# DeltaNet block inversion: the unknown begun as the identity on the chip, and the inverse kept row first in memory

## What is computed

```
A = where(strict, einsum('bhnid,bhnjd->bhnij', kb, k) * decay, 0.0)
eye = jnp.eye(C)
rhs = concatenate([v * beta, kb * exp(g)], -1)
sol = triangular_solve(eye + A, rhs, left_side=True, lower=True, unit_diagonal=True)
```

## Time and profile before

| | us |
|---|---|
| median of 3 runs | 952.81 |
| the three runs | 952.17, 952.81, 958.84 |
| span of the profiled execution, first to last instruction | 950.6 |
| DeltaNet heads 0 to 7, first join (L1472) of head 0 to that of head 7 | 428.98 to 718.35 |
| mean granted clock of TensorE over the span | 0.888 of full speed |

### The profile page before, as it was taken

How to read it: one execution, slowest core, us unless ns; L and a number is a source line. 1 busy time by engine, 2 the same in 40 slices (tenths; PEclk the granted TensorE clock), 3 DMA queues, 4 the chain that set the end, 5 groups by cost and what they waited for, 6 DMA issues and landing times. The chain is left out here.

```text
span 950.6 us, 14976 instructions
## 1 busy us (share of the span) xinstructions
PE 775.6 (82%) x5209; PEld 466.6 (49%) x5209; DVE 429.6 (45%) x1039; ACT 336.3 (35%) x776; POOL 290.3 (31%) x694
## 2 busy tenths in 40 slices
PE   0978869999999178999998989989987646999970
PEld 0644425555555024456656666656655333555540
DVE  0039543212122583634765767665844652112116
ACT  0231322322222225534755556464631121322221
POOL 0000112333333100455272735537260012333330
PEclk9989959999999569986998999997997757999995
DMA  9999999999791798657242351523210199999913
GB/s 234 406 375 400 407 382 380 383 366 336 258 378 57 308 362 246 204 157 227 40 117 67 89 140 33 140 44 113 46 50 7 62 408 360 361 379 385 374 69 124
DMA packets 115874, 220.47 MB, mean 232 GB/s; under 512 B 44631, under 2 KB 78751, under 8 KB 104801
## 3 DMA queue, kind: packets, MB, share of 16 engines
q1 hardware_dynamic: 106847, 201.56, 61.0%
q0 software_dynamic: 8224, 15.75, 4.9%
q10 hardware_dynamic: 740, 2.32, 0.8%
HBM read 213.27 MB, written 17.33 MB: 243 GB/s over the span
## 5 line engine op out<-in xcount | busy, mean ns | idle before, releaser
L1200 PE MATMUL banks<-h_cols,weight_ring 128*128 128x512 f32 (+1 forms) x384 | 166.7, 556 | 0.8
L809 DVE TENSOR_TENSOR arena<-arena,banks 128x128 f32<-128x128 f32 x42 | 12.1, 287 | 203.7 <-ACT arena L780 203.7
L867 POOL DMA_INDIRECT y_of_tokens<-arena,place_now x42 | 44.0, 1048 | 169.7 <-ACT arena L787 169.7
L1200 PEld LDWEIGHTS banks<-h_cols,weight_ring 128*128 128x128 f32 x384 | 69.8, 205 | 35.6 <-issue 32.0
L1182 POOL TENSOR_TENSOR arena<-arena 128x60 f32<-128x60 f32 (+10 forms) x240 | 78.7, 328 | 18.8
L1180 POOL TENSOR_TENSOR arena<-arena 128x60 f32<-128x60 f32 (+10 forms) x240 | 76.5, 319 | 18.8
L287 PE MATMUL banks<-weight_ring,c_cols 128*32 128x512 f32 x368 | 53.0, 694 | 27.8 <-DMA weight_ring<-in_w_mod_dram 27.8
L845 POOL DMA_INDIRECT arena<-h_of_tokens,row_now x50 | 49.2, 984 | 85.9 <-DVE place_of_slot L714 38.0
L775 ACT COPY arena<-arena 64x1024 f32<-64x1024 f32 x46 | 48.1, 1045 | 77.1 <-PE banks L733 56.8
L752 PE MATMUL banks<-weight_ring,arena 128*64 128x256 f32 x576 | 67.6, 389 | 1.1 <-ACT arena L775 1.1
L733 PE MATMUL banks<-const,arena 64*128 64x64 f32 x352 | 57.1, 285 | 13.1 <-ACT arena L775 13.1
(11 more groups left out here) (294 smaller groups left out, 1395.2 us busy)
## 6 DMA issues: line engine op xcount, KB each, us to landing
weight_ring<-in_w_mod_dram SPq DMA_DIRECT2D x46, 1024.0 KB, 9.5
weight_ring<-in_dn_w_in_dram SPq DMA_DIRECT2D x32, 512.0 KB, 7.1
weight_ring<-in_w_gate_dram SPq DMA_DIRECT2D x13, 1024.0 KB, 11.1
weight_ring<-in_w_up_dram SPq DMA_DIRECT2D x13, 1024.0 KB, 14.4
weight_ring<-in_w_down_dram SPq DMA_DIRECT2D x13, 1024.0 KB, 16.1
arena<-in_w_gate_dram SPq DMA_DIRECT2D x7, 1024.0 KB, 11.5
arena<-in_w_up_dram SPq DMA_DIRECT2D x7, 1024.0 KB, 14.0
arena<-in_w_down_dram SPq DMA_DIRECT2D x7, 1024.0 KB, 15.4
```

The costliest lines, as they stand in the source:

```text
L867: pool.indirect_dma_start(y_halves, bass.IndirectOffsetOnAxis(m.place_now[:, u:u + 1], 0), v.y_tile[u], None, bounds_check=last_row, oob_i ...
L1200: mm = pe.matmul(bank(6 + j % 2)[:, 0:CTX + SEQ - n0], head_w[h % 2][:, j, k, :], m.hT[:, k, n0:CTX + SEQ], start=(k == 0), stop=(k == KD ...
```

## The change

U is no longer loaded: GpSimd copies the identity (in U's layout) into it, after the previous head's U has been written out and before it waits for the loads, which are now four. The elimination runs over columns 0 to 30 rather than 1 to 30, so that it begins with the identity and ends as the inverse: 31 pairs instead of 30, with q = j // 4 + 1 row groups instead of (j - 1) // 4 + 1. The mask and the closing subtraction are gone. The inverse lies in memory as (block, row, system, column) instead of (system, block, row, column), so that the load of W_diag reads one run of 1 KB for each partition. The mask leaves the constants, which shrink from 16 to 14 column blocks of 64 KB.

```diff
-C_STRICT, C_EYE = 11, 13
+C_EYE = 11
-C_SLOT = 15
-N_CONST = 16
+C_SLOT = 13
+N_CONST = 14
...
-        w_dram = nc.dram_tensor("inverted_blocks", (SYS, NB, BLK, BLK), F32).ap()
+        w_dram = nc.dram_tensor("inverted_blocks", (NB, BLK, SYS, BLK), F32).ap()
...
         def sp_blocks_in(sp, h):
             sp.wait_ge(s("n_out"), 16 * (h + 1))
-            sp.dma_start(U, n_dram.rearrange("s k (q g) c -> g (s k) q c", g=4)).then_inc(s("m_in"), 16)
             for g in range(4):
                 sp.dma_start(M[g * BLK:(g + 1) * BLK, :, :], n_dram.rearrange("s k r c -> (s k) r c")).then_inc(s("m_in"), 16)
 
         def sp_inverse_out(sp, h):
             sp.wait_ge(s("block_step"), STEPS * (h + 1))
-            sp.dma_start(w_dram.rearrange("s k (q g) c -> g (s k) q c", g=4), U).then_inc(s("u_out"), 16)
+            sp.dma_start(w_dram.rearrange("k (q g) s c -> g s k q c", g=4), U).then_inc(s("u_out"), 16)
...
-            sp.dma_start(W_diag, w_dram.rearrange("s k r c -> (k r) s c")).then_inc(s("w_base"), 16)
-
-        STEPS = 2 + 2 * (BLK - 2)
+            sp.dma_start(W_diag, w_dram.rearrange("k r s c -> (k r) s c")).then_inc(s("w_base"), 16)
+
+        STEPS = 1 + 2 * (BLK - 1)
...
-            pool.wait_ge(s("m_in"), 80 * (h + 1))
-            then(pool.tensor_tensor(U, U, v.strict_rows, ALU.mult))
-            for j in range(1, BLK - 1):
-                q = (j - 1) // 4 + 1
+            if h >= 1:
+                pool.wait_ge(s("u_out"), 16 * h)
+            then(pool.tensor_copy(U, v.eye_rows))
+            pool.wait_ge(s("m_in"), 64 * (h + 1))
+            for j in range(BLK - 1):
+                q = j // 4 + 1
                 part = U_part[:, 0:q, 0:BLK - 1 - j]
                 then(pool.tensor_tensor(part, U[:, 0:q, j:j + 1].to_broadcast([P, q, BLK - 1 - j]),
                                         M[:, j, j + 1:BLK].unsqueeze(1).to_broadcast([P, q, BLK - 1 - j]), ALU.mult))
-                then(pool.tensor_tensor(U[:, 0:q, j + 1:BLK], U[:, 0:q, j + 1:BLK], part, ALU.subtract))
-            pool.tensor_tensor(U, v.eye_rows, U, ALU.subtract).then_inc(s("block_step"), 1)
+                ins = pool.tensor_tensor(U[:, 0:q, j + 1:BLK], U[:, 0:q, j + 1:BLK], part, ALU.subtract)
+                if j < BLK - 2:
+                    then(ins)
+                else:
+                    ins.then_inc(s("block_step"), 1)
...
-                sp.wait_ge(s("m_in"), 80 * (x + 2))
+                sp.wait_ge(s("m_in"), 64 * (x + 2))
```

More of the change, by code:

```diff
@@ L114, in columns @@
     v.lower_in = c[:, C_LOWER_IN * P:(C_LOWER_IN + 1) * P]
-    v.strict_rows = c[:, C_STRICT * P:(C_STRICT + 2) * P].rearrange("p (q n) -> p q n", q=8)
     v.eye_rows = c[:, C_EYE * P:(C_EYE + 2) * P].rearrange("p (q n) -> p q n", q=8)
@@ L2319, in constants @@
     row = 4 * (np.arange(2 * P)[None, :] // 32) + i // 32
-    put(C_STRICT, np.arange(2 * P)[None, :] % 32 > row)
     put(C_EYE, np.arange(2 * P)[None, :] % 32 == row)
```

## The result

| | before | changed |
|---|---|---|
| median, us | 952.49 (4 runs) | 927.88 (4 runs: 927.07 to 931.07) |
| ratio of the runs | | 0.9732, interval 0.97 to 0.9764 |
| span of the profiled execution | 950.6 | 929.2 |
| same, five more rounds: median | 954.05 (9 runs) | 929.29 (5 runs), ratio 0.9728, 0.9702 to 0.9755 |

Faster by 24.6 us, where 18.4 were forecast.

The account below looks back on a forecast made before the run. Bound: the inversion's turn through SP, memory and GpSimd, just above TensorE's need. Head 2 3.2, four stretches 13.5, last stretch 1.4, constants 0.3: 18.4 us off span 950.6, 932.2, plus 2.2: 934.4 us; 8-in-10 range 931.5 to 944.5.

Parts of the forecast that it names:

- The saving per turn: Inversion loop, from one N_diag write to the next, 41.07 us in head 2: 3.2 us less forecast.
- The load of U: SP's loads before GpSimd starts: dropping U's issue saves 0.6 us and M's hold 1.8, together 2.4 per turn.
- The hold: One M load issue per head held to 2.4 us, blamed on U's 1024 small pieces filling the queue: 1.82 us.
- the upper bound: Load of U, at most 3.5 us saved per turn, if M also lands faster, by 1.1 us.
- Rival 1: M, not U, lands late; the 2.4 us hold is M's own: 1.4 saved per turn, 943.4 us, chance 0.13.
- GpSimd: 0.4 forecast: Elimination per turn: mask and subtraction gone, one pair and wider row groups added, 0.6 saved, less 0.2 for VectorE's disturbance.
- W_diag's 0.4: Back-load of W_diag in 128 runs of 1 KB for 1024 of 128 B: 0.4 us saved per turn.
- The floor of TensorE: Stretch between joins: TensorE alone needs 37.9 us; 38.15 with VectorE's floor, 38.3 with a residue.
- The 0.25 for VectorE's extra work: Steps 3 to 6: VectorE's transposes finish at 552.2, 0.25 us after TensorE is ready for the join.
- "Saving more than 3.5 per turn brings only 1 us more": Whole kernel: beyond 3.5 us saved per turn TensorE is the bound, so only 1 us more is gained.
- Rival 4: Clock still falls after 1 us waits, or GpSimd slows: two or three stretches stay at 40, 940 us, chance 0.09.
- A step that no row shows: Write of U in the new layout, 4.86 us to SP's next issue: 0 saved, bounds 0 and -2.7.

Follow-up runs that it names:

- the dead load: Changed kernel with U's removed load put back, issued ahead of M's four into U_part, which GpSimd overwrites: 935.9 us, ratio 0.9833.
- the changed kernel's second profile: The changed kernel run again with no edit, five more rounds: ratio 0.9728 against the kernel before, span 923.4 us.

## Why the prediction was wrong, and where it was right

**The saving per turn otherwise.** The load of U: 3.06 us for 2.4 forecast, and its mechanism as told. The hold belonged to U's load (back with the dead load, gone without), and M also landed faster after its last issue (2.8 us to GpSimd's start in head 2, from 3.8), which I had in the upper bound alone. So GpSimd started 4.1 us after SP's first M, where I had named 4.5 to 5.5. Rival 1 fell with it. GpSimd: 0.4 forecast, -0.10 measured. Counting instructions was not enough: the time from GpSimd's start to U's write did not get shorter. In head 7, beside a quieter VectorE, it is 24.2 before and 23.8 after, but 24.1 in the changed kernel's second profile and 23.7 in the kernel with the new layout alone, whose GpSimd work is the old one. So no gain of GpSimd is shown, and why it is missing stays open. W_diag's 0.4 is real (2.1 us to landing, from 2.5), but I put it into the turn, where SP does not wait for it.

**The floor of TensorE.** I took 37.9 us, plus 0.25 and a residue, for what TensorE needs, and called 38.3. It was 37.1 to 37.6. The 37.9 held a wait of 0.28 us inside it, for VectorE, which was late since the decay rows were queued behind SP's wait for M; with M early that went too, and 0.3 to 0.5 us more for which no row names a cause. I had listed those loads as going out 2 to 3 us earlier, and gave them no gain. The 0.25 for VectorE's extra work was right: the joins of heads 3 to 6 wait 0.2 to 0.4 us.

**How it adds up.** With a write of 4.8 us the turn is 38.2 to 38.9 and still just above TensorE: 936.5, a saving of 1.9% where 18.4 us are 1.9%. So the forecast was near for a change without the faster write, and partly by luck: the load of U gave more than I took, GpSimd and W_diag nothing in the turn, and my floor was above TensorE's. With the faster write the turn falls below TensorE's work, the joins' waits go and five stretches fall to the floor: 7 to 8 us more. "Saving more than 3.5 per turn brings only 1 us more" was wrong by that floor.

**The clock.** No join waited over 0.5 us and the clock stayed full, as forecast. Rival 4 had something: waits of 1.57 and 1.71 us were each followed by one stretch at 0.88 and 41.0 us long, while others, up to 1.62 us, were not. Such a stretch costs 2 us more than its neighbours (41.0 beside 38.9), so part of the gain between 3 and 5 us saved per turn is the clock's.

**What stays open.** The stage gives 22.3 us; the medians differ by 24.6 and 24.8. After head 7's join the changed kernel took 231.4 and 230.6 us, the one before 232.2, so 1 to 1.6 may lie there; but over all kernels here that part scatters between 230.6 and 233.3, and the part ahead by 5 us, so no cause is shown for the rest.

## What to carry to other kernels

When a transfer's layout changes, merge its access pattern by hand before pricing it: two dimensions at one common step become one, and the length of the outermost then can decide the rate. A step that no row shows needs a bound on the side of a gain too. And a stretch taken as an engine's own need must be searched for short waits, since what is freed elsewhere may free them as well.

## What the runs showed of the hardware

A load of 1024 pieces of 128 bytes, outer length 4, held the next DMA of its queue in every head: that issue took 2.18 to 2.45 us with it ahead and 0.32 without it. Behind the same load split in four it took 0.60 us, in one head 1.45. Another of M's four issues was now and then long as well (1.3 to 1.9 us, in one or two heads of seven traces), with that load ahead and without, and no run shows why. The same 128 KB written in pieces of 128 bytes took 4.93 us to the next issue with an outer length of 4, 2.63 with 32, and 3.95 in four writes; the pieces moved at 45 GB/s in the first and at 131 in the second, and 4, 16 and 64 packets of 4 bytes stood at the ends. GpSimd's copy of 128x256 took 0.40 us, its two-input operation of that shape 0.72. After waits of 2.8 to 3.6 us TensorE ran part of the time that followed at 1.2 instead of 2.4 GHz (granted clock 0.84 to 0.96); with the waits filled by useless products the clock was 1.00 throughout. Waits of 1.57 and 1.71 us were followed by 0.88, others up to 1.62 by 1.00, and in two kernels the clock fell (0.91 and 0.96) in stretches whose join had not waited at all.
